# Gathers re-timed, gate stores in four pieces, and one layer's gate matrices in another PSUM layout

## The reference, cut to what matters

```python
top_s, top_i = lax.top_k(sc, PEER_TOPK)               # 16 best of 128 keys, for 8 heads x 2 halves
cand = top_s[:, :, 0, :, None] + top_s[:, :, 1, None, :]
best_s, best_pos = lax.top_k(cand.reshape(t, PEER_HEADS, PEER_TOPK * PEER_TOPK), PEER_TOPK)
experts = i1 * N_KEYS + i2
gates = jax.nn.softmax(best_s, axis=-1).astype(h.dtype)
act = jnp.einsum('thkd,td->thk', u_tab[eb], hb)       # rows of u of the chosen experts
coef = gb * jax.nn.gelu(act, approximate=False)
out = jnp.einsum('thk,thkd->td', coef, v_tab[eb])     # rows of v of the chosen experts
```

## Time and profile before

| | |
|---|---|
| median of 3 runs | 2868.51 us (2867.86 to 2872.08) |
| the profiled execution | 2868.51 us, its span 2866.8 us |
| mean granted TensorE clock | 0.998 of full speed |
| busy: PE, DVE, ACT, POOL | 2810.2, 2495.0, 1370.3, 949.7 us |
| DMA | 855.05 MB, 298 GB/s over the span |
| gate matmuls, L1588 | 1408, 106.0 us busy |
| u tiles in layer 0 | about 400 to 960 us of the span |
| u tiles in layer 1 | about 1791 to 2353 us of the span |

### The profile page before, as it was taken

How to read it: one execution, slowest core, us unless ns; L and a number is a source line. 1 busy time by engine, 2 the same in 40 slices (tenths; PEclk the granted TensorE clock), 3 DMA queues, 4 the chain that set the end, 5 groups by cost and what they waited for, 6 DMA issues and landing times.

```text
span 2866.8 us, 49322 instructions
## 1 busy us (share of the span) xinstructions
PE 2810.2 (98%) x17864; PEld 2602.4 (91%) x17864; DVE 2495.0 (87%) x5020; ACT 1370.3 (48%) x2321; POOL 949.7 (33%) x773
## 2 busy tenths in 40 slices
PE   7999999999999999999999999999999999999998
PEld 4777789999999999999988788999999999999998
DVE  4667788999999799999987679999999979999998
ACT  3345124367777333334353532445777753333433
POOL 1000028733335244444400000684333434444342
PEclk9999999999999999999999999999999999999999
DMA  7434748989999899999932122698999999999996
GB/s 278 173 118 176 261 143 306 342 331 396 391 374 348 336 378 386 382 383 384 378 123 74 59 74 82 225 327 323 386 377 390 363 339 363 383 379 386 382 382 252
DMA packets 257143, 855.05 MB, mean 298 GB/s; under 512 B 26080, under 2 KB 59104, under 8 KB 250336
## 3 DMA queue, kind: packets, MB, share of 16 engines
q1 hardware_dynamic: 149280, 442.23, 41.9%
q0 software_dynamic: 98496, 381.73, 35.3%
q10 hardware_dynamic: 9216, 29.36, 2.5%
HBM read 777.06 MB, written 76.15 MB: 298 GB/s over the span
## 4 chain that ended last, share of the span: by engine, by line
PE 82%; DMA 6%; DVE 5%; ACT 3%; issue 2%; POOL 1%; SPq 0%; DVEq 0%; ACTq 0%; POOLq 0%
PE banks L1092 43%; PE banks L1627 27%; DMA w_raw<-wst 4%; PE banks L1588 3%; PE banks L1425 2%; DVE w_lo L1668 2%; ACT w_hi L806 1%; PE banks L1162 1%; PE banks L1108 1%; PE banks L1512 1%; DMA pj<-adaw 1%; DVE vacc L2180 1%; POOL w_lo L755 1%; PE banks L1266 0%; DMA activations<-act_out 0%
## 5 line engine op out<-in xcount | busy, mean ns | idle before, releaser
L806 ACT ACTIVATE w_hi<-w_raw 128x1024 fp32r<-128x1024 f32 x596 | 630.8, 1059 | 778.6 <-PE banks L1092 635.2
L1092 PE MATMUL banks<-hH,w_hi 128*128 128x352 f32 (+1 forms) x2528 | 873.4, 345 | 18.0 <-issue 9.0
L1668 DVE TENSOR_TENSOR w_lo<-w_raw,w_hi 128x1024 fp32r<-128x1024 f32 x522 | 638.4, 1223 | 254.2 <-ACT w_hi L806 238.2
L1092 PE MATMUL banks<-hH,w_lo 128*128 128x352 f32 (+1 forms) x2528 | 849.0, 336 | 0.0
L1092 PE MATMUL banks<-hL,w_hi 128*128 128x352 f32 (+1 forms) x2528 | 848.7, 336 | 0.0
L768 POOL DMA_INDIRECT ring<-v,gidx x320 | 393.6, 1230 | 627.1 <-DVE vacc L2180 536.5
L1092 PEld LDWEIGHTS banks<-hH,w_hi 128*128 128x128 f32 x2528 | 474.8, 188 | 68.3 <-issue 38.2
L1627 PE MATMUL banks<-c_lo_late,w_hi 128*128 128x352 f32 x1536 | 493.9, 322 | 0.0
L1092 PEld LDWEIGHTS banks<-hH,w_lo 128*128 128x128 f32 x2528 | 474.3, 188 | 19.5
L1092 PEld LDWEIGHTS banks<-hL,w_hi 128*128 128x128 f32 x2528 | 475.3, 188 | 17.3 <-issue 0.5
L768 POOL DMA_INDIRECT ring<-u,gidx x244 | 280.5, 1150 | 461.3 <-DVE gact L2168 441.8
(11 more groups left out here) (354 smaller groups left out, 3957.2 us busy)
## 6 DMA issues: line engine op xcount, KB each, us to landing
w_raw<-wst SPq DMA_DIRECT2D x596, 512.0 KB
activations<-act_out SPq DMA_DIRECT2D x124, 352.0 KB
act_in<-activations SPq DMA_DIRECT2D x62, 704.0 KB
gate_matrices<-stages ACTq DMA_DIRECT2D x64, 448.0 KB
gates<-gate_matrices SPq DMA_DIRECT2D x64, 448.0 KB
ada_buf<-adaw POOLq DMA_DIRECT2D x24, 1024.0 KB, 7.2
nrm<-adaw POOLq DMA_DIRECT2D x8, 1024.0 KB, 5.1
pj<-adaw POOLq DMA_DIRECT2D x7, 1024.0 KB, 7.3
```

The lines of the kernel that those rows point to most:

```text
L806: nc.scalar.activation(w_hi[g % 2][:, :, :].rearrange("p a b -> p (a b)"), w_raw[:, g % RAWS, :], ACT.Copy).then_inc(s_wh, 1)
L1092: last = mm(bank[s][:, 0:t.stop - t.start], a[s][:, k, :], b[:, k, t], start=(k == 0 and a is w_hi and b is hH), stop=(k == KT - 1 and a i ...
L1668: v.tensor_tensor(w_lo[g % 2][:, :, :].rearrange("p a b -> p (a b)"), w_raw[:, g % RAWS, :], w_hi[g % 2][:, :, :].rearrange("p a b -> p (a ...
```

## The change

Four things change, all of them in the u tiles.

1. STORES is 4 and not 8: each chunk is stored in 4 stores of 896 KB after 4 tiles, not in 8 of 448 KB after 8.
2. GpSimd's issues during tiles 10 to 38: before, one behind each tile from 10 on and two behind every third (39 in all); now one behind tiles 11 to 31, 33 to 35, 37 and 38 (26). AHEAD is 30 and not 38.
3. DVE's gathers. Early ones: before 4, 11 and 14 in the rounds tt = 1, 2, 3 (29), now 6, 7 and 7 (20), with two ahead of each pick. From tile 37 on the counts come from another rule. By stretch of tiles:

| tiles | 37 | 38 to 41 | 42 to 54 | 55 to 104 | 105 to 119 | 120 to 126 |
|---|---|---|---|---|---|---|
| before | 1 | 8 | 22 | 68 | 27 | 5 |
| now | 2 | 8 | 20 | 75 | 23 | 12 |

4. In layer 1 alone the bank of a quad is seen as expert x token: a matmul writes its 128 values 4 places (16 bytes) apart, and ACT reads the bank in a row. Layer 0 keeps its layout.

The diff:

```diff
-STORES = 8
+STORES = 4
...
-EARLY_GATHERS = ((0, 0, 0, 0), (0, 0, 0, 4), (0, 3, 3, 5), (3, 4, 4, 3))
-EARLY = sum(sum(early) for early in EARLY_GATHERS)
-AHEAD = 38
+EARLY_GATHERS = (0, 6, 7, 7)
+EARLY = sum(EARLY_GATHERS)
+AHEAD = 30
...
-POOL_GATHERS = [0] * N_KEYS
-for _n in range(10, GATHER0 + 2):
-    POOL_GATHERS[_n] = 2 if _n % 3 == 1 else 1
+POOL_GATHER_AT = [11, 12, 13, 14, 15, 16, 17, 18, 19, 20, 21, 22, 23, 24, 25, 26, 27, 28, 29, 30, 31, 33, 34, 35, 37, 38]
...
-GATHER_RATES = ((GATE0, 55, 170), (55, 105, 138), (105, GATE1, 173), (GATE1, N_KEYS - 3, 100))
...
+for _n in range(GATE0, N_KEYS - 1):
+    U_GATHERS[_n] = 1 if len(quads_of(_n + 1)) > 1 or _n == N_KEYS - 2 or _n % 2 and _n % 3 and _n + 1 < GATE1 else 2
+for _n in range(N_KEYS - 4, GATE0, -9):
+    U_GATHERS[_n] -= sum(U_GATHERS) > UG - EARLY and U_GATHERS[_n] > 1
...
-        def by_expert(q):
-
-            return bank[2 + q % 2][:, :].rearrange("p (t e) -> p e t", t=QUAD)
+        def by_expert(l, q):
+
+            return bank[2 + q % 2][:, :].rearrange("p (t e) -> p e t" if l == 0 else "p (e t) -> p e t", t=QUAD)
...
-                    for _ in range(POOL_GATHERS[n - U0]):
-                        gather(l, k)
-                        k += 1
-                for k in range(sum(POOL_GATHERS), GATHERS):
+                    if n - U0 in POOL_GATHER_AT:
+                        gather(l, POOL_GATHER_AT.index(n - U0))
+                for k in range(len(POOL_GATHER_AT), GATHERS):
                     gather(l, k)
...
+                    early = EARLY_GATHERS[tt]
                     if tt == 1:
                         dve.wait_ge(s_htr, l + 1)
                     for a in range(2):
-                        early_gathers(EARLY_GATHERS[tt][1 + a])
+                        for _ in range(early // 3):
+                            gather_u(gathered)
+                            gathered += 1
                         picked(tt, a)
-                    early_gathers(EARLY_GATHERS[tt][3])
+                    for _ in range(early - 2 * (early // 3)):
+                        gather_u(gathered)
+                        gathered += 1
                     gated(tt)
```

More of the change, by code:

```diff
@@ L157 @@
 AHEAD_SET = 4
-POOL_GATHERS = [0] * N_KEYS
-for _n in range(10, GATHER0 + 2):
-    POOL_GATHERS[_n] = 2 if _n % 3 == 1 else 1
+POOL_GATHER_AT = [11, 12, 13, 14, 15, 16, 17, 18, 19, 20, 21, 22, 23, 24, 25, 26, 27, 28, 29, 30, 31, 33, 34, 35, 37, 38]
 U_GATHERS = [0] * N_KEYS
 for _n in range(GATHER0, GATE0):
-    U_GATHERS[_n] = 2 if _n > GATHER0 else 1
-assert EARLY + sum(U_GATHERS) == AHEAD and sum(POOL_GATHERS) <= AHEAD + RING
-GATHER_RATES = ((GATE0, 55, 170), (55, 105, 138), (105, GATE1, 173), (GATE1, N_KEYS - 3, 100))
[L166 to L171, removed]
+    U_GATHERS[_n] = 2
+assert EARLY + sum(U_GATHERS) == AHEAD and len(POOL_GATHER_AT) <= AHEAD and POOL_GATHER_AT[-1] < GATHER0 + 2
+for _n in range(GATE0, N_KEYS - 1):
+    U_GATHERS[_n] = 1 if len(quads_of(_n + 1)) > 1 or _n == N_KEYS - 2 or _n % 2 and _n % 3 and _n + 1 < GATE1 else 2
+for _n in range(N_KEYS - 4, GATE0, -9):
+    U_GATHERS[_n] -= sum(U_GATHERS) > UG - EARLY and U_GATHERS[_n] > 1
 assert sum(U_GATHERS) + EARLY == UG and U_GATHERS[N_KEYS - 1] == 0, (UG - EARLY, sum(U_GATHERS))
@@ L777, in _ @@
                         load_ada(1, c)
-                k = 0
                 for n in range(POOL_LO0, POOL_LO1):
@@ L782, in _ @@
                     lo(l, n)
-                    if n - U0 == POOL_GATHERS.index(max(POOL_GATHERS)):
+                    if n - U0 == POOL_GATHER_AT[0]:
                         if l == 0:
@@ L1047, in _ @@
                         nc.scalar.activation(
-                            home[:, :, i * QUAD:(i + 1) * QUAD], by_expert(q),
+                            home[:, :, i * QUAD:(i + 1) * QUAD], by_expert(l, q),
                             ACT.Copy, scale=2.0 ** -GATE_UP).then_inc(s_gv, 1)
@@ L1587, in gate_quad @@
                         for part in range(2):
-                            last = mm(by_expert(u)[:, :, t], oh[:, 2 + part, t, :], oh[:, 1, t, :].bitcast(BF16),
+                            last = mm(by_expert(l, u)[:, :, t], oh[:, 2 + part, t, :], oh[:, 1, t, :].bitcast(BF16),
                                       start=(part == 0), stop=(part == 1))
@@ L2334, in _ @@
                 gathered = 0
[L2336 to L2340, removed]
                 for tt in range(NT):
@@ L2344, in _ @@
                     candidates(tt)
-                    early_gathers(EARLY_GATHERS[tt][0])
                     best_pairs()
```

## The result

| | before | after |
|---|---|---|
| median | 2870.3 us (2867.9 to 2876.8) | 2919.2 us (2910.6 to 2924.0) |
| span of the profiled execution | 2866.8 us | 2916.8 us |
| mean granted TensorE clock | 0.998 | 0.995 |

What follows compares the result with a forecast made beforehand. The prediction took TensorE, busy 98% of the span, as the bound; its terms -11 + 0.8 + 2.2 - 1 + 2 + 8 + 38.7 = +39.7 on 2868.5 us gave 2908 us, range 2859 to 2918.

Steps and rivals of the forecast that it cites:

- A: Routing, tiles 10 to 38: GpSimd issues one gather after a tile, never two, so TensorE's idle time there goes; -11 us.
- B: Routing: gathers landing in sets of four come later, DVE waits, scores reach ACT 0.9 us late; +0.8 us for both layers.
- C: Hand-over at tile 37: two gathers instead of one on the path from DVE to TensorE; +2.2 us.
- C2: DVE's gathers in the middle, tiles 42 to 119: fewer at both ends, seven more in tiles 55 to 104, covered; -1 us.
- D: Four store bursts a layer take bandwidth from the weights and activations queue, mostly covered by weight buffers; +2 us (0 to +10).
- E: End of the u tiles, 120 to 126: seven more gathers in a stretch already on DMAs, about half replaced; +8 us.
- F: Layer 1's quads: matmuls writing 16 bytes apart take 55 ns more each, 704 of them; +38.7 us (bounds 0 and +64).
- the sum: GpSimd in tiles 10 to 38: four gathers and three subtractions take 12.60 us where three tiles take 11.76.

Runs made afterwards that it cites:

- e5: The kernel before with only the new gather lists of after (8 stores a chunk, old bank layout): ratio 1.0000.
- e12: e9 with GpSimd's 26 issues doubled at every third tile, from tile 11 to 35, none later than with single issues: ratio 0.9997.
- e13: e9 with GpSimd's 26 single issues starting at tile 12 and not 11, none at tile 32: ratio 1.0027.
- e3: The kernel before with only 4 stores of 896 KB a chunk, one after each tile, and not 8 of 448 KB: ratio 1.0075.
- e9: e5 with one gather at tile 37, an eighth early one in the last round, and seven gathers moved from tiles 120 to 126 to the middle: ratio 0.9977.
- e1: The kernel before with only layer 1's quad matmuls writing their 128 values 16 bytes apart: 2908.2 us, ratio 1.0132.
- e7: The kernel before with 4 stores of 896 KB a chunk, one after every second tile and not after each: ratio 1.0001.
- e11: e9 with a single GpSimd issue behind every tile from 10 to 38, 29 and not 26: 2858.8 us, ratio 0.9964.
- e6: The kernel before with only layer 1's quad matmuls writing their values 8 bytes apart: 2908.0 us, ratio 1.0137.

## Why the prediction was right and wrong

| term | forecast | found | by |
|---|---|---|---|
| A, doubled issues | -11 | -11.3 to -11.5 | after, e5; e12 |
| B, sets of four | +0.8 | 0 | after; margin by e13 |
| C, hand-over | +2.2 | +3.0, in after +5.6 (clock) | e5, after |
| C2, middle | -1 | -1.6 | e5 |
| D, stores | +2 | +20.8 alone, some +9 in after | e3 |
| E, end | +8 | +7.9, in after +8.7 | e5, e9 |
| F, the step | +38.7 | +38.3 | e1 |

**F** is right in place and, by luck in part, in size: 47 ns a matmul (0.37 us / 8) and not 55 gives 32.6, and 5.7 come from the slower pace of the u matmuls, which I had seen nowhere. The sign came true, 0.89 us a quad where I wrote 0.9. The choice between ends of 0 and +64 by the nearest row was the weak step and held.

**A** has the right size, by luck in part; its cause is the single delay and not the sum. Where the earlier trace rows has an idle piece after every third tile, the chain of after is one piece of TensorE from 440 to 489 us:

```profile
440.00 49.05 PE banks L1085 x297
```

**B** is just covered, as forecast: DVE's first early gather and its shifted scores in after, then ACT:

```profile
463.53 1.22 DVE L2161 CUSTOM_DVE_ANT_0 stages<-stages,banks 128x1024 f32<-128x1024 f32 x1 [12.69 <-DMA stages<-u,gidx]
...
491.83 0.29 DVE L2254 TENSOR_TENSOR bestv<-bestv,banks 128x128 f32<-128x128 f32 x1
```

```profile
492.15 0.31 ACT L1020 ACTIVATE bestv<-bestv 128x128 f32<-128x128 f32 x1 [0.30 <-DVE bestv L2254]
...
494.26 1.06 ACT L799 ACTIVATE w_hi<-w_raw 128x1024 fp32r<-128x1024 f32 x1 [1.22 <-PE banks L1085]
```

12.7 us of idle DVE (12 forecast), scores at 491.8 (491.1), ACT waits 0.30 us (0.9 forecast) with 1.22 to spare against 1.51 before.

**C** had the idle time right (1.94 us, 1.9 forecast); I had not counted that the clock can fall behind it.

**The clock** is in no term. In before's u tiles it never falls; in after's trace it falls six times, at 561, 656, 834, 963, 1967 and 2394 us, each time behind an idle TensorE of 1.8 to 3.4 us. At the 1.6 us measured at the hand-over they come to some 10 us of the 50, an estimate, spread over C, D and E.

**D is the step that failed**. Its working had two parts. The first was "if three full queues share alike the 413 GB/s, it gets 138": it got 114, since, as I read the counts, they shared alike in packets and the change doubled the size of one queue's. (The 0.19 in that sum should read 0.019 MB a us; 0.5 MB and 3 us a burst are right.) The second weighed more: 3 us in each of four bursts in two layers are 24 us, and I took all but 2 as covered by three buffers of weights. The term alone is +20.8, above its bound of +10. Late weights were covered as far as e7 has them (7.2 us), late stores of activations were not, and two falls of the clock a layer came on top (e3). The rule of the Trainium skill that I set against it (DMA: Bandwidth & Descriptors, Measured), transfers of at least 1 MiB, is about how fast a transfer itself goes and misled here: 896 KB in place of 448 KB gained nothing (e7) and at the same pace of issue cost 22.5 us (e3). In layer 1 the slower quads hide D: after's gate stretch (35.3) has even less than F alone (38.3), as its tiles up to about 60 still go at the faster pace. That D is hidden fits a tile of 4.88 us, in which q1 needs 0.70 / 4.88 = 143 GB/s and not 157.

**E** is right, though its chain of DMAs reads differently than forecast. After, layer 0, answering to the earlier trace rows:

```profile
933.89 9.55 DMA ring<-u,gidx
...
946.29 15.40 DMA activations<-act_out
```

The sum was 10 us short: D by 7, C by 3.4. The one execution at a clock of 0.999 lies 40.3 us above before, nearly the forecast's 39.7; with D priced at 2 that is luck.

## What to carry to other kernels

A layout that made TensorE write with gaps cost about 0.37 us per eight 128-column matmuls, at a step of 8 as of 16 bytes, so let the engine with time to spare take the jumps. When transfers of several queues meet, count packets and their size, not only bytes: here larger and as frequent pieces of the least urgent stream took bandwidth from the most urgent one. Before issues are moved later or put in pairs, look for the one that a whole set waits for and for the margin behind it; here 0.3 us of waiting were free, and 6.7 cost 15 over both layers. A wait of TensorE of some 2 us can cost 1.6 us above its length, since the clock can fall behind it; one of 5 us cost 2.7 more (e13). The version with single issues, one gather at tile 37 and the old end of the u tiles (e11) runs at 2858.8 us, 0.9964 of the kernel before.

## What the runs showed of the hardware that I had not expected

- The 352-column matmuls of a tile run at one of two paces, 3.81 to 3.87 or 3.99 to 4.04 us per 24, at a granted clock of 1.00 both times. With quads written in a row tiles alternate; with a step all of them went slow (e1, e6). What sets the pace stays open.
- TensorE's granted clock fell to 0.57 for some 4 us behind a wait of 1.94 us in after, and did not behind the same wait in e5. Behind 4.99 us in e13 it was 0.51 for 6.9 us.
- A matmul written with a step lasts 89 ns longer (311 against 222), but sets back what follows by only 47.
